# Second block of a two-block transformer kernel: both attentions set between halves of the projection units

## The reference: what is computed

```python
h = rms(x, attn_norm)
c_q, c_kv, k_rope, dq, dk, dv, g_mla, g_diff = split(h @ w_in)        # 256,256,32,1024,1024,1024,1024,1024
q  = rms(c_q) @ w_uq ; kv = rms(c_kv) @ w_ukv                          # 16 heads of 96; of 64 + 64
k_nope, v_mla = kv[:64], kv[64:]; k = concat(k_nope, k_rope)           # same k_rope for all heads
q, k = rope(rms_head(q)), rope(rms_head(k))
o_mla = softmax(q k^T / sqrt(96)) v_mla                                # no mask, 256 x 256 a head
qd, kd = rms_head(dq), rms_head(dk)                                    # 8 heads, two maps each
a1, a2 = softmax(qd_i kd_i^T / 8 - slope * |pos_q - pos_k|)
o_diff = rms_head((a1 - lam * a2) vd) * (1 - lam_init)
merged = sigmoid(g_mla + b) * o_mla + sigmoid(g_diff + b) * o_diff
x = x + merged @ w_out
h2 = rms(x, ffn_norm)
# 16 experts, each takes the 32 tokens with the highest router score for it (softmax over experts, top 32)
y = (silu(xe @ w_gate_e) * (xe @ w_up_e)) @ w_down_e * gate            # w_gate, w_up 1024 x 2048, w_down 2048 x 1024
out = x + scatter_add(y)
```

## Time and profile before

| | us |
|---|---|
| median of three executions | 1938.32 |
| the profiled execution | 1939.98 |
| its span | 1938.2 |
| second block up to the end of its output projection | 674 to 1001.4 |
| first expert matmul | 1025.89 |
| TensorE busy in the span | 1506.3 (78%) |

### The profile page before, as it was taken

The page is one execution under the profiler, slowest core; times in us unless marked ns, Lnnn a source line. Parts: engine busy times, 40 slices in busy tenths (PEclk is TensorE's granted clock), DMA queues, the critical chain, the costliest instruction groups (busy, mean ns, idle before and its releaser), DMA issues.

```text
span 1938.2 us, 25846 instructions
## 1 busy us (share of the span) xinstructions
PE 1506.3 (78%) x11156; PEld 1027.1 (53%) x11174; DVE 625.5 (32%) x980; ACT 529.8 (27%) x868; POOL 134.0 (7%) x151
## 2 busy tenths in 40 slices
PE   7999999999999997899888565566656565655655
PEld 7887999887999897789564111112211111111111
DVE  5666444566444544455762000000000000000000
ACT  6445434545343555435631000000000000000000
POOL 0251000031000003410200000000000000000000
PEclk9999999999999989999999878777777878788877
DMA  8443555433555434213098999999999999999997
GB/s 264 149 148 119 189 177 191 153 131 123 182 193 176 140 116 123 87 48 131 1 414 342 428 427 427 428 428 428 427 427 428 429 427 426 429 427 428 427 427 320
DMA packets 138705, 542.01 MB, mean 280 GB/s; under 512 B 10109, under 2 KB 103506, under 8 KB 113906
## 3 DMA queue, kind: packets, MB, share of 16 engines
q1 hardware_dynamic: 138562, 540.50, 70.9%
q0 software_dynamic: 48, 0.13, 0.0%
HBM read 539.56 MB, written 1.05 MB: 279 GB/s over the span
## 4 chain that ended last, share of the span: by engine, by line
PE 46%; DMA 42%; DVE 5%; ACT 3%; POOL 2%; issue 1%; SPq 0%; DVEq 0%; ACTq 0%; POOLq 0%
DMA ew<-in_expert_w_up_dram 16%; DMA ew<-in_expert_w_gate_dram 14%; DMA ew<-in_expert_w_down_dram 12%; PE bank L1090 11%; PE bank L1091 11%; PE bank L1092 11%; PE bank L1584 3%; PE bank L1609 1%; PE bank L1097 1%; DVE wL L1630 1%; POOL arena L679 1%; PE bank L1111 1%; PE bank L1174 1%; PE bank L1313 1%; ACT wH L722 1%
## 5 line engine op out<-in xcount | busy, mean ns | idle before, releaser
L1584 PE MATMUL bank<-ew,xeT 128*32 128x512 f32 x2048 | 337.3, 794 | 233.4 <-DMA ew<-in_expert_w_up_dram 127.2
L1630 DVE TENSOR_TENSOR wL<-ring,wH 128x2048 fp32r<-128x2048 f32 x128 | 294.7, 2302 | 271.9 <-ACT wH L722 271.5
L1584 PEld LDWEIGHTS bank<-ew,xeT 128*32 128x32 f32 x2048 | 64.4, 128 | 490.4 <-DMA ew<-in_expert_w_up_dram 207.5
L722 ACT ACTIVATE wH<-ring 128x2048 fp32r<-128x2048 f32 x128 | 244.4, 1910 | 285.7 <-PE bank L1092 282.6
L1090 PE MATMUL bank<-xH,wH 128*128 128x256 f32 x1056 | 302.9, 287 | 7.6 <-DVE wL L1630 7.0
L1091 PE MATMUL bank<-xL,wH 128*128 128x256 f32 x1056 | 299.2, 283 | 0.0
L1092 PE MATMUL bank<-xH,wL 128*128 128x256 f32 x1056 | 299.1, 283 | 0.0
L1609 PE MATMUL bank<-ew,tok 128*32 128x256 f32 x2048 | 168.7, 488 | 107.2 <-DMA ew<-in_expert_w_down_dram 100.3
L1090 PEld LDWEIGHTS bank<-xH,wH 128*128 128x128 f32 x1056 | 202.8, 192 | 14.4 <-issue 9.0
L1091 PEld LDWEIGHTS bank<-xL,wH 128*128 128x128 f32 x1056 | 202.9, 192 | 0.8
L1092 PEld LDWEIGHTS bank<-xH,wL 128*128 128x128 f32 x1056 | 202.8, 192 | 0.0
(11 more groups left out here) (292 smaller groups left out, 1780.0 us busy)
## 6 DMA issues: line engine op xcount, KB each, us to landing
ew<-in_expert_w_gate_dram SPq DMA_DIRECT2D x64, 2048.0 KB, 45.9
ew<-in_expert_w_up_dram SPq DMA_DIRECT2D x64, 2048.0 KB, 46.3
ew<-in_expert_w_down_dram SPq DMA_DIRECT2D x63, 2048.0 KB, 46.0
ring<-in_w_gate_up_dram SPq DMA_DIRECT2D x44, 1024.0 KB, 5.0
ring<-in_w_down_dram SPq DMA_DIRECT2D x22, 1024.0 KB, 4.9
ring<-in_w_in_dram SPq DMA_DIRECT2D x22, 1024.0 KB, 5.2
ring<-in_w_out_dram SPq DMA_DIRECT2D x12, 1024.0 KB, 4.9
ring<-in_w_in_fox_dram SPq DMA_DIRECT2D x10, 1024.0 KB, 9.3
```

The lines of the kernel that those rows point to most:

```text
L722: act.activation(wH[:, n % 2, w], ring[:, slot(n), w], ACT.Copy).then_inc(w_hi, 1)
L1584: mm = pe.matmul(bank[half][32 * j:32 * j + 32, :], xeT[:, k, CAP * e:CAP * e + CAP], w_[:, m, 512 * j:512 * j + 512], start=(k == 0), sto ...
L1630: dve.tensor_tensor(wL[:, n % 2, w], ring[:, slot(n), w], wH[:, n % 2, w].bitcast(F32), ALU.subtract).then_inc(w_split, 1)
```

## The change

The second block is written anew; the arithmetic that each product needs stays. (1) A new order of units (ORDER2): c, dq0, uq, ukv, dq1 to dq3, ga0 come ahead of the MLA attention; nine units (dk, ga1 to ga3, dv0, dv1) are put half by half into its 16 steps; six (dv2, dv3, gb) into 12 of the 16 steps of the diff attention. All zero matmuls of both attentions are gone. (2) The values product of MLA writes its output already turned and two heads at a time (as in the first block), so `turn_outputs("mla")` is gone. (3) Norms are folded: the reciprocal root of q's head sums goes into the exponential (`scale` and `bias` by row), that of k into its tile with the already rotated `k_rope`; the rope of q is on VectorE, squares of k, dq and dk and the scaling of dq and dk on GpSimd. (4) The gates use tanh (0.5 folded into bias, softmax scale and sub-norm weight) in place of sigmoid. (5) Norm and merge of the diff output are done in two batches, the first inside the last steps, where the first output unit is run too. (6) Expert loads start in another order of slots. (7) The nine norm rows are loaded from ScalarE's queue. (8) Rope angles and lambda are computed inside the first layer's attention, the sines before the second layer's.

```diff
-        c_u = units(2)
...
-        diff_u = units(12)
+        ORDER2 = ("c0", "c1", "dq0", "uq0", "uq1", "ukv0", "ukv1", "dq1", "dq2", "dq3", "ga0",
+                  "dk0", "dk1", "ga1", "dk2", "dk3", "ga2", "ga3", "dv0", "dv1",
+                  "dv2", "dv3", "gb0", "gb1", "gb2", "gb3")
...
+        FILL2 = ORDER2[11:]
+        PARTS2 = [(name, j) for name in FILL2 for j in range(2)]
+        MLA_FILL = [PARTS2[0:2], PARTS2[2:4]] + [[p] for p in PARTS2[4:18]]
+        DIF_STEPS = 16
+        DIF_FILL = dict(zip((0, 1, 3, 4, 5, 7, 8, 9, 11, 12, 13, 15), PARTS2[18:]))
...
@@ ScalarE @@
+            def vec(r, src, n):
+                act.dma_start(vrows[r:r + n, :], src).then_inc(vec_in, 16)
...
-                        act.activation(dst(u)[:, j, :], b2(u)[:, j, :], ACT.Sigmoid,
-                                       bias=row(ROW["bgate"] + c)).then_inc(gate_ev, 1)
...
+                    act.activation(to[:, j, :], b2(b)[:, j, :], ACT.Tanh, bias=row(ROW["bgate"] + c0 + 2 * u + j),
+                                   scale=0.5).then_inc((gate_ev, fill_ev)[j], 1)
...
+                    act.activation(p_sb[:, m % 4, :], bank[j][:, 0:S], ACT.Exp, bias=rms[:, m:m + 1],
+                                   scale=rstd[:, rs:rs + 1], accum_out=rsum[:, m:m + 1]).then_inc(lay["exp"], 1)
+                for name in fill_done(MLA_FILL[i]):
+                    high(U2[name] + 2)
+                    fill_out(name)
...
+                if d == 12:
+                    sub_root(0)
+                    preload(ACT.Exp)
+                if d == 15:
+                    merged_high(0)
+                    merged_high(1)
+            high(wout2_u[0] + 2)
+            sub_square(3)
+            sub_root(1)
+            high(wout2_u[1] + 2)
+            merged_high(2)
+            merged_high(3)
...
@@ TensorE @@
-            BUSY = {"mla": 2, "dif": 2}
-
-            FILL = (0, 8, 6)
...
+            for i in range(16):
+                c, qt = i // 2, i % 2
+                pe.wait_ge(lay["exp"], lay_at(MLA, "exp", 2 * i))
+                for j in range(2):
+                    mm = pe.matmul(bank[j][:, 0:S], qTm[0:MLA_QK, 2 * c + j, P * qt:P * qt + P],
+                                   kTm[0:MLA_QK, 2 * c + j, :], start=True, stop=True)
+                mm.then_inc(lay["score"], 1)
+                if i >= 3 and i % 2 == 1:
...
+                    mla_pv((i - 3) // 2)
+                fill_half(*MLA_FILL[i][0])
+                if i > 0:
+                    mla_turn(i - 1)
+                for part in MLA_FILL[i][1:]:
+                    fill_half(*part)
+                if i in (13, 15):
+                    pe.wait_ge(dn_mul, 4 if i == 13 else 8)
+                    for b in (0, 1) if i == 13 else (2, 3):
+                        turn_diff(b)
...
-            keep_busy(16, 4)
-            turn_outputs("dif", 4, sn_mul)
-            out_proj(wout2_u, mTL, 0, 1)
+                if d == 14:
+                    turn_outputs(0)
+                if d == 16:
...
+                    out_part(0, 0)
+                if d == 17:
+                    out_part(0, 1)
+            pe.wait_ge(w_split, wout2_u[1] + 1)
+            out_part(1, 0)
+            out_part(1, 1)
+            turn_outputs(1)
...
@@ VectorE @@
+                    if L == 0 and i == 6:
+                        angles()
...
+                if i > 0 and MLA_FILL[i - 1][-1][1] == 1:
+                    low(U2[MLA_FILL[i - 1][-1][0]] + 2)
+                mla_scale(i)
+                if i >= 3 and i % 2 == 1:
+                    mla_gated((i - 3) // 2)
+                if i > 0:
+                    mla_turned(i - 1)
+                if i == 3:
+                    diff_sums(0)
...
@@ SyncE @@
-            for g in range(4):
-                load_expert(0, g)
...
+            sp.wait_ge(w_split, NU - 4)
+            load_expert(0, 0)
+            sp.wait_ge(w_split, NU - 2)
+            load_expert(0, 1)
+            sp.wait_ge(lay["pv"], lay_at(DIF, "pv", DIF_STEPS))
+            load_expert(0, 2)
...
+            sp.wait_ge(w_used, NU)
+            for g in range(6, ESLOTS):
                 load_expert(0, g)
```

More of the change, by code:

```diff
@@ L198, in build @@
[L198 to L210, removed]
+        c_tok = view(15360, NT, 512)
@@ new lines, in build @@
+        sq = [view(8192 + 1536 * t, MLA_H, MLA_QK) for t in range(NT)]
+        v_mla = tok[:, :, :]
+        gaT = mT = view(2048, KD, S)
+        dk_tok = view(4096, NT, 16, HD)
+        gbT = view(4096, KD, S)
+        v_d = view(6144, NT, D)
+        dqT = view(8192, DIFF_H, S)
+        posr_i = view(12288, S).bitcast(I32)
+        posr_f = view(12544, S)
+        absd = view(12800, NT, S)
+        mH = view(0, KD, S, split=True)
+        mL = view(10240, KD, S, split=True)
+        small = bias_sb[:, :, :].rearrange("p a b -> p (a b)")
@@ L1425, in _ @@
             mm.then_inc(kr_mm, 1)
-            pe.wait_ge(c_hat, 4)
+            unit_mm(U2["dq0"], halves(4), "T", which=(0,))
+            pe.wait_ge(c_dve, 5)
             for b in range(2):
@@ new lines, in _, with fill_half @@
+            unit_mm(U2["ga0"], halves(3), "F")
+            pe.wait_ge(k_mul, 4)
+            for b in range(8):
+                if b < 4:
+                    pe.wait_ge(turn_a, 5 + b)
+                elif b % 2 == 0:
+                    pe.wait_ge(turn_a, 8 + (b - 4) // 2 + 1)
+                else:
+                    pe.wait_ge(turn_d, (b - 4) // 2 + 1)
+                turn_heads(1, b)
+            pe.wait_ge(dproj_ev, 4)
+            def fill_half(name, j):
+                if j == 0 and FILL2.index(name) >= 2:
+                    pe.wait_ge(fill_ev, EV[FILL2[FILL2.index(name) - 2]])
+                unit_mm(U2[name], halves(fill_bank(name)), "F" if name[0] == "g" else "T", which=(j,))
@@ L1495, in _ @@
[L1495 to L1515 removed]
+                            hd = 2 * b + j
@@ new lines, in per_head @@
+            def per_head(a, at, width):
+                return a[:, at:at + 16].rearrange("p (h a) -> p h a", a=1).broadcast_to([P, 16, width])
+            values_out(0)
+            low(U2["dq1"])
+            for t in range(NT):
+                dve.wait_ge(q_sq, t + 1)
+                dve.tensor_reduce(ss[:, 16 * t:16 * t + 16], sq[t], X, ALU.add).then_inc(sums, 1)
+            low(U2["dq2"])
+            values_out(1)
+            dve.wait_ge(rope_t, 4)
+            dve.wait_ge(kr_ss, 3)
@@ new lines, in _ @@
+            rope(0)
+            low(U2["dq3"])
+            rope(1)
+            for t in range(NT):
+                dve.wait_ge(squared, t + 1)
+                dve.tensor_reduce(ss[:, 32 + 16 * t:48 + 16 * t], head_sq(t), X, ALU.add).then_inc(sums, 1)
+            low(U2["ga0"])
+            dve.wait_ge(roots, 1)
+            dve.wait_ge(roots, 3)
+            dve.reciprocal(rstd[:, :], rms[:, :]).then_inc(qk_rinv, 1)
+            dve.wait_ge(qk_rinv, 1)
+            dve.wait_ge(kr_step, 4)
```

1104 lines of the change are left out of this document (589 added, 515 removed).

## The result

| | before | changed |
|---|---|---|
| median, us | 1938.40 (1936.79 to 1939.36) | 1912.26 (1904.34 to 1914.34) |
| ratio | | 0.9856, interval 0.9839 to 0.9872 |
| profiled execution, span | 1939.98, 1938.2 | 1904.34, 1902.6 |
| first unit of the first block | 17.71 | 15.13 |
| c projection starts | 673.3 | 667.6 |

The change is worth 26 us in the medians, where I had forecast 52 (1886, range 1867 to 1909; the median lies 3 us above it).

The account below looks back on a forecast made before the run. Experts were bound by weight reads, earlier work by TensorE. The second block gains 69.5 + 4 - 25.5 = 48, plus 2.3 and 2.4 makes 52.7 less: 1886 us, range 1867 to 1909.

Parts of the forecast that it names:

- What bounds the kernel, and that the end follows the first expert matmul: Experts bound by weight reads, TensorE before them; the end moves one to one with the first expert matmul.
- What goes, 69.5 us: Second block, 696.2 to 1001.4: idle 38.35, zero matmuls 21.5, MLA values 7.7 and output turning 1.97 disappear.
- Of the clock ... I take 4: Second block: removing long gaps lets TensorE's clock recover, giving back 0 to 9 us, taken as 4.
- so they count in full: 100 zero matmuls in the MLA and diff attentions stand in order on TensorE, so removing them saves 21.5 us.
- New waits, 25.5: Second block: new TensorE waits ahead of MLA 5, dk/dq turnings 3, MLA steps 5, diff 9, end 3.5.
- the scaling stands behind the split in order: MLA steps: VectorE's work, about 8 of 9.7 us per two steps, fits on average but cannot run ahead; waits 5.
- GpSimd beside VectorE ... 0.6 us a split: GpSimd's squares and scalings beside nine weight splits lengthen each by no more than 0.6 us, within the 25.5.
- The rival of VectorE as the bound (1906): Attention steps: 15 splits ahead of the scaling delay the turning in full, 20 us more, 1906; chance 0.18.
- The rival of the clock: Interleaved MLA and diff steps: short waits lower the granted clock; at half the work the time is 1961; chance 0.05.
- Start and first feed-forward, 4.7: Norm rows on ScalarE's queue gain 2.3 at the start; angles and lambda moved from the first feed-forward gain 2.4.

Follow-up runs that it names:

- the second profile: The changed kernel run once more with nothing altered; its profiled execution took 1913.78 us, the run's median 1910.92 us, ratio 0.9855 to the kernel before.
- The version with no falls in the second block of its profile: Changed kernel plus copy ahead of scaling, dq/dk squares on ScalarE, k_rope's matmuls spread, 66 zero matmuls in remaining waits, run again: 1887.50 us, ratio 0.9722.

## Why the prediction was wrong

- *What bounds the kernel, and that the end follows the first expert matmul:* right (912.3 and 911.4 us behind it; no load came late).
- *What goes, 69.5 us:* the instructions went. Zeros, values and turning were to shorten TensorE's busy time by 31.2 us, and by 35.2 with the clock; it was 26.1.
- *"Of the clock ... I take 4":* this step failed. I let long gaps go and the clock recover, while the zeros, which had kept it up in the waits, went as well. In the profiled execution the clock gave nothing back, it took some 2.5 us; in the second profile, which is near the median, busy time is 4.7 us longer still and the block starts 3.1 later, at the same waits. That profile accounts for the whole miss: it has 13.8 us of busy time and 10.7 of waits more than forecast, and the block starts 2.2 later; that is 26.7, and 1913.78 lies 26.5 above 1887.3. Zeros put into the new waits gave 12 us back, and 35 at the end alone 6 to 7. I had also misread the 0.89: my window began at 696.20, in a fall that had begun at 687 in the block of k_rope, before any gap. Of 22.4 us at the lower level in that window TensorE was busy for 13.4, and this fall did not go with the gaps (6.8 and 10.2 us of it in the changed kernel's profiles).
- *"so they count in full", 21.5 us for the zeros:* too high as priced: the kernel before without them gains 8. Of the 12.5 us of zeros behind the first diff score 5.4 came back as waits, for which the forecast had a term, and 6.4 as clock, for which it had none.
- *New waits, 25.5:* this step failed too; it was 35.9. Before MLA 5.5 for 5, diff steps 7.3 for 9. MLA with dq and dk 14.6 for 8: the two turnings 3.6 for 3, but inside the steps 11.0 for 5, of which the copy behind the scaling and GpSimd's hold are 8.3. I had named that "the scaling stands behind the split in order", but not that the copy stands behind the scaling. The end 8.5 for 3.5: I had counted one split each for two waits (4.0 and 4.5), and the norm, turning, merge, split chain is passed twice.
- *"GpSimd beside VectorE ... 0.6 us a split":* failed in kind. The rule that I cited and set aside was right: it is not the split that grows by half a microsecond but a short scaling that is held 3.1 us.
- *The rival of VectorE as the bound (1906):* its amount was no matter (72 of 107 us), its order was. Its time is nearer to 1912 than my own, and that is luck: its price was for splits that delay the turning.
- *The rival of the clock:* I gave it 0.05 as an all or nothing case, from short gaps in the diff window at 0.99. It came true in part: from the c projection to the end of the output projection TensorE was busy at the lower level for 34.9 us (44.7 in the second profile), where it had been for 29.2.
- *Start and first feed-forward, 4.7:* the first profile shows 5.7 at the c projection (17.71 to 15.13, and the 2.9 us wait gone), the second 2.6, for the clock fell at 666, and undoing either edit does not make the kernel slower. Traced waits of 2 to 3 us aren't gains while the clock's falls move by more than that.

## What to carry to other kernels

Price a wait twice: its length, and what TensorE runs at the lower clock behind it; and before taking fillers out, ask what keeps the clock where they stood. Before promising a fall of the clock back, look in which instructions it began: not every one begins in a gap. In an engine's program put what another engine waits for ahead of what can be held: moving one copy before a scaling gave 13 us with no work saved. When a second engine works on the same side of the memory, look for a short instruction that is held by a long one, not for a long one that grows a little.

## What was not expected of the hardware

- VectorE's scaling of 2 x 256 elements with one input took 3.69 us for 0.62 while GpSimd squared twice 1024 elements, and 1.13 when the squares were cut in four.
- TensorE's clock fell inside a block of back-to-back matmuls of 32 columns, 6.0 and 4.6 us after its start in two profiles, with no idle time in the 4 us windows around (4.00 of 4.00 busy at 0.50), and in none of seven profiles in which the same matmuls stood between ones of 256 columns. The kernel before had it too (0.77 granted in 673 to 700).
- One kernel's executions differ by 10 us (1904.34 to 1914.34); in the two that were profiled (1904.34 and 1913.78) the waits are the same and the clock falls at other places. The version with no falls in the second block of its profile still spread by 4 to 5 us (1883.57 to 1888.77); that profile has 10.2 us at the lower level in three falls ahead of the block.
